# Attention of a two-layer trunk: the reciprocal sum moves from the exponentials to the matrix that they are transposed with

## The chip, the cores and the metric

The kernel runs on one core of a Trainium2 chip. The metric is the device time of one execution in microseconds, the lower the better. PE is the matrix engine (PEld its weight loads, which the profile shows on their own), DVE the vector engine, ACT the scalar engine, POOL the GpSimd engine, SP the engine that issues most DMAs. The matrix engine has two clock levels, 1.2 and 2.4 GHz; the granted clock is given as a share of the higher one.

## The reference, cut to what matters

A trunk of two layers over 256 latent and 256 context tokens of width 1024. Layer 0 mixes tokens by Fourier groups and a bidirectional state-space scan, layer 1 by attention; each is followed by a squared-ReLU MLP of width 4096. Only the attention of layer 1 is touched. It has 16 heads of 64: 8 window heads (4 query heads share one key head, a band mask, and a sink logit that takes part in the sum but has no value vector) and 8 neighbourhood heads (a bias per pair of positions). Every latent query sees the 256 latent and the 256 context keys:

```
s_loc  = where(valid, q k^T * scale, NEG_INF)      # or + bias
s_ctx  = q kc^T * scale
p      = softmax(concat([s_loc, s_ctx, s_sink], -1), -1)
o      = p_loc @ v + p_ctx @ vc
```

So a row of 512 exponentials is divided by its sum, and the result multiplies the values. All of it is in 32-bit floats.

## The kernel before

The kernel is written by hand, engine by engine. The function `script()` returns one list of steps. Every engine walks that same list and emits its own part of each step in that order, with semaphores between engines; nothing reorders instructions afterwards. For every result in PSUM (the eight banks that the matrix engine writes) a small table names the bank, what fills it and what frees it.

The attention is cut into 16 units, `ATTN`: a pair of heads (`par` 0 and 1) by one of two blocks of 128 queries. Index `i` below is the unit, 0 to 15; units 0 to 7 are window heads, 8 to 15 neighbourhood heads. The steps of a unit are:

- S (PE, L2383): scores of both heads, 128 queries by 512 keys, one PSUM bank each. Four banks are used in turn, two per unit.
- max (DVE, L1882 to L1893): adds mask or bias in PSUM, takes the row maximum, turns its sign.
- exp (ACT, L1393): reads the bank, writes `prob` (128 queries by 512 keys in SBUF, three units deep) as exp(s - max) and the row sum beside it.
- scale (DVE, L1902, L1905, L1909): adds the sink (window heads), takes the reciprocal, and multiplies `prob` of each head in place by it, one instruction of 128x512 per head, `prob_done` + 1 for each.
- PT (PE, L2392): for each head four transposes of 128x128, so that keys lie on partitions. `prob` is loaded as the weights, the identity matrix streams past. One bank per head (2 and 3).
- PT on ACT (L1404): copies both banks to `pT` in SBUF.
- O (PE, L2410): values times `pT`, four chunks of keys for each head, the two heads beside each other in the array.
- ohi, olo (ACT L1408, DVE L1914): every second unit, splits the output into a high and a low part for the output projection.

In the steady part one round of the script, for `j`, reads

```
for kind, i in (("S", j + 2), ("ohi", j - 2), ("max", j + 1), ("scale", j), ("olo", j - 2), ("exp", j + 1), ("PT", j), ("O", j - 1)):
```

so PE runs S of unit j+2, PT of unit j, O of unit j-1; DVE runs max of j+1, scale of j and, every second round, olo; ACT runs ohi, exp of j+1 and the copies of PT of j. The first units start beside the input projection of the layer, whose last products (L1936) end shortly before. When the attention ends, PE makes a row of gate values (L2222, step `grow`) and the output projection and the second MLP follow, in which nearly all products are of the three-fold form at L1936 and L1943.

Two other places use the matrix engine on plain 32-bit operands of the size that matters here. In layer 0, step `y` ends with three products whose moving operand is the identity, added into a bank (L2204), in each of 16 steps:

```
ins = mm(ps[:, b, P * i:P * i + P], ycomb[:, n % 2, P * i:P * i + P], ident, start=False, stop=True, skip_group_check=True)
```

and step `cb` makes four products of 128x128 by 128x128 in each of 4 steps (L2168), directly after the transposes of step `toks` (L2151, L2152; `nc.tensor.transpose`, as in PT).

Of the kernel before, what the change touches and what calls it, by code (L numbers as in the profile page):

```python
# [14 lines left out]
ALU = mybir.AluOpType  # L15
# [5 lines left out]
P = 128  # L21
# [3 lines left out]
T = SEQ + CTX  # L25
# [336 lines left out]
def trunk(nc, x, ctx, w_mod, vectors, w_ff1, w_ff2, w_in_even, w_dt, w_out_even, w_in_odd, rpb_na, w_out_odd,  # L362
# [171 lines left out]
    with ExitStack() as stack:  # L534
# [114 lines left out]
        bias = place("bias", [P, 2, 8, SEQ], offset=region + 16384)  # L649
        prob = place("prob", [P, 3, 2, T], offset=macc_at + 7680)  # L650
        pT = place("pT", [P, 2, 2, T], offset=vtok_end)
        assert vtok_end + 8 * 2 * T <= region + 16384
        fin = place("fin", [P, 2, D], offset=out_at)
        grow = place("grow", [P, D], offset=out_at + 2 * 4 * D)

# [10 lines left out]
        for name, w in (("cos", SEQ), ("sin", SEQ), ("perm", P), ("dup0", P), ("dup1", P), ("heads", P),  # L666
# [31 lines left out]
                 "wdthi_done wdtlo_done dtv_done dte_done dtln_done dt_done dtx_done uf_done vf_done pad_done acc_done "  # L698
                 "th_done xbc_done hs_done btok_done xdt_done xw_done ent_done seg_done g_done y_done zt_done gate_done gated "
                 "ysq_done mix_done mixhi_done hr_done hq_done hidhi_done hid_done qraw_done qn_done rope_done "  # L700
                 "vT_done vtok_done kd_done max_done exp_done rs_done prob_done pT_done pv_done ohi_done "
                 "tap_done xskip_done fin_done out_in vhi_done vsplit_done pair_used zr_done cvec_done crow_done ccol_done shift_done shh_done shl_done uo_done ahi_done").split()
        S = {n: sem(n) for n in names}
        (arow_done, rows_out, coef_half, grow_done, htok_done, unit_done, sines_done, hv_done, mfull_done, dtrow_done, acc_sq, tmp_sq, mu_used, row_done, mcol_done, modc_done, sil_done, hi_done, lo_done, c0_in, dft_in, xsq_done, xrms_done, xr_done, xn_done, xnt_done, xu_done, c1_in, vec_in, wdt_in, bias_in, dve_seq, act_seq,
# [2 lines left out]
         uf_done, vf_done, pad_done, acc_done, th_done, xbc_done, hs_done, btok_done, xdt_done, xw_done, ent_done, seg_done,  # L707
         g_done, y_done, zt_done, gate_done, gated, ysq_done, mix_done, mixhi_done, hr_done, hq_done, hidhi_done,
         hid_done, qraw_done, qn_done, rope_done, vT_done, vtok_done, kd_done, max_done,
         exp_done, rs_done, prob_done, pT_done, pv_done, ohi_done, tap_done, xskip_done, fin_done, out_in, vhi_done, vsplit_done, pair_used, zr_done, cvec_done, crow_done, ccol_done, shift_done, shh_done, shl_done, uo_done, ahi_done) = (S[n] for n in names)  # L710
        x_in = [sem(f"x_in{t}") for t in range(NCH)]

        def signalled(what):
# [698 lines left out]
        def _(dve):  # L1412
# [51 lines left out]
            for st in steps:  # L1464
# [371 lines left out]
                elif k == "hnorm":  # L1836
                    dve.wait_ge(hs_done, qk_n[st[1:]] + 1)
                    dve.wait_ge(qraw_done, qk_n[st[1:]] + 1)
                    x_ = ktile(*st[1:])
                    key = ("hstat",) + st[1:]  # L1840
                    r_, b = rms_of(key), jobs[key][0]
                    c_ = u32[:, 0, 0:odd_tokens[st[1:]]]
                    if qk_n[st[1:]]:
                        dve.wait_ge(qn_done, qk_n[st[1:]])
                    v.tensor_tensor(c_, r_, r_, ALU.mult).then_inc(signal(dve_seq), 1)
                    dve.wait_ge(*latest())
                    v.scalar_tensor_tensor(out=c_, in0=ps[:, b, 0:odd_tokens[st[1:]]], scalar=HD * EPS, in1=c_, op0=ALU.add, op1=ALU.mult).then_inc(signal(hv_done), 1)
                    v.scalar_tensor_tensor(out=x_, in0=x_, scalar=vt[:, 2, g_q[st[1]]:g_q[st[1]] + 1],
                                           in1=r_, op0=ALU.mult, op1=ALU.mult).then_inc(signal(dve_seq), 1)
                    dve.wait_ge(hv_done, qk_n[st[1:]] + 1)  # L1850
                    v.tensor_scalar(c_, c_, -0.5 / HD, 1.5, ALU.mult, ALU.add).then_inc(signal(dve_seq), 1)
                    dve.wait_ge(*latest())
                    v.tensor_tensor(x_, x_, c_, ALU.mult).then_inc(signal(qn_done), 1)
                elif k == "rot":
                    x_ = ktile(*st[1:])[:, 0:SEQ]
                    b = jobs[st][0]
                    dve.wait_ge(*filled(st))
                    dve.wait_ge(*latest())
                    v.tensor_tensor(rp[:, 0, :], x_, cuts["cos"], ALU.mult).then_inc(signal(dve_seq), 1)
                    v.tensor_tensor(rp[:, 1, :], ps[:, b, 0:SEQ], cuts["sin"], ALU.mult).then_inc(freeing(st), 1)  # L1860
                    dve.wait_ge(*latest())
                    v.tensor_tensor(x_, rp[:, 0, :], rp[:, 1, :], ALU.add).then_inc(signal(rope_done), 1)
                elif k == "dup":
                    b = jobs[st][0]
                    dve.wait_ge(*filled(st))
                    v.tensor_copy(kdup[:, st[1], :], ps[:, b, :]).then_inc(signal(kd_done), 1)
                elif k == "max":
                    i = st[1]
                    t, qt = ATTN[i]
                    b = jobs[st_S(i, 0)][0]  # L1870
                    for par in range(2):
                        dve.wait_ge(*filled(st_S(i, par)))
                    if t < 4:
                        o = P * (1 - qt)
                        cut_ = ps[:, b:b + 2, o:o + P]
                        add = cuts["win"][:, None, P * qt:P * qt + P].broadcast_to([P, 2, P])
                    else:
                        if t == 4:
                            dve.wait_ge(bias_in, 16 * 8)
                        cut_ = ps[:, b:b + 2, 0:SEQ]  # L1880
                        add = bias[:, qt, 2 * (t - 4):2 * (t - 4) + 2, :]
                    v.tensor_tensor(cut_, cut_, add, ALU.add).then_inc(signal(dve_seq), 1)  # L1882
                    dve.wait_ge(*latest())
                    v.tensor_reduce(sm[:, 3, i % 3, :], ps[:, b:b + 2, :], AX, ALU.max).then_inc(signal(dve_seq), 1)  # L1884
                    dve.wait_ge(*latest())
                    if t < 4:
                        sinks = bc[:, 120 + 2 * t:122 + 2 * t]
                        v.tensor_tensor(sm[:, 3, i % 3, :], sm[:, 3, i % 3, :], sinks, ALU.max).then_inc(signal(dve_seq), 1)
                        dve.wait_ge(*latest())
                        v.tensor_scalar(sm[:, 0, i % 3, :], sm[:, 3, i % 3, :], -1.0, None, ALU.mult).then_inc(signal(dve_seq), 1)  # L1890
                        v.tensor_tensor(sm[:, 4, i % 3, :], sinks, sm[:, 3, i % 3, :], ALU.subtract).then_inc(signal(max_done), 1)
                    else:
                        v.tensor_scalar(sm[:, 0, i % 3, :], sm[:, 3, i % 3, :], -1.0, None, ALU.mult).then_inc(signal(max_done), 1)  # L1893
                elif k == "scale":
                    i = st[1]
                    t, qt = ATTN[i]
                    row = lambda r: sm[:, r, i % 3, :]
                    for par in range(2):
                        dve.wait_ge(*exponential_done(i, par))
                    src = row(1)  # L1900
                    if t < 4:
                        v.tensor_tensor(row(5), row(1), row(2), ALU.add).then_inc(signal(dve_seq), 1)  # L1902
                        dve.wait_ge(*latest())
                        src = row(5)
                    v.reciprocal(row(4), src).then_inc(signal(rs_done), 1)  # L1905
                    dve.wait_ge(*latest())
                    for par in range(2):
                        pr = prob[:, i % 3, par, :]
                        v.tensor_scalar(pr, pr, sm[:, 4, i % 3, par:par + 1], None, ALU.mult).then_inc(signal(prob_done), 1)  # L1909
                elif k == "olo":  # L1910
                    t = st[1]
                    dve.wait_ge(ohi_done, t + 1)
                    b, _ = jobs[("Opair", t)]
                    v.tensor_tensor(a_lo[:, t, 0:SEQ], ps[:, b, 0:SEQ], a_hi[:, t, 0:SEQ].bitcast(F32), ALU.subtract).then_inc(signal(split_done), 1)  # L1914
                elif k == "out":
                    dve.wait_ge(grow_done, 2)
                    dve.wait_ge(htok_done, 4)
                    for q in range(4):
                        t, c_ = q // 2, 512 * (q % 2)
                        dve.wait_ge(*filled(("acc", q)))  # L1920
                        v.tensor_tensor(nt[:, q % 2, :], ps[:, B_TOK[q], :], grow[:, c_:c_ + 512], ALU.mult).then_inc(signal(dve_seq), 1)
                        dve.wait_ge(*latest())
                        v.tensor_tensor(fin[:, t, c_:c_ + 512], nt[:, q % 2, :], fin[:, t, c_:c_ + 512], ALU.add).then_inc(signal(fin_done), 1)
# [3 lines left out]
        def _(pe):  # L1927
# [42 lines left out]
            for st in steps:  # L1970
# [413 lines left out]
                elif k == "PT":  # L2384
                    i = st[1]
                    for par in range(2):
                        pe.wait_ge(prob_done, 2 * i + par + 1)
                        b = jobs[st + (par,)][0]
                        if free_before[st + (par,)]:
                            pe.wait_ge(*emptied(st + (par,)))  # L2390
                        for kk in range(NCH):
                            ins = nc.tensor.transpose(ps[:, b, P * kk:P * kk + P], prob[:, i % 3, par, P * kk:P * kk + P], ident)  # L2392
                        ins.then_inc(filling(st + (par,)), 1)
                elif k == "O":
                    i = st[1]
# [89 lines left out]
```

## Time and profile before

| | us |
|---|---|
| median of 3 runs | 1194.53 |
| lowest, highest | 1194.1, 1195.05 |
| the profiled execution, its own time | 1193.66 |
| its span, first to last instruction | 1191.9 |

Of the span PE is busy 1159.9 us (97%), its weight loads 930.6 (78%), DVE 840.6 (71%), ACT 616.9 (52%), POOL 84.4 (7%). Matmuls are pipelined: a row of the trace gives the time from a matmul's start to its modelled end, which overlaps the next one, so the distance between starts says more than the duration. Times inside the span are microseconds from its start. In a timeline, neighbouring instructions of one kind are merged into a row: start, length, engine, line, operands, how many (x), and in brackets the idle time of the engine before it with what ended it.

### The profile page before, as it was taken

What the parts mean: (1) busy time and instruction counts of PE and PEld (TensorE: products, weight loads), DVE (VectorE), ACT (ScalarE), POOL (GpSimd) and SP (SyncE); (2) the same over time, 40 slices, a digit from 0 to 9 for tenths busy, and PEclk for the clock granted to TensorE, in tenths of its full rate; (3) what the DMA queues carried; (4) which work ended last, traced back from release to release, by engine and by line L of the source; (5) the groups of instructions that cost most, each with busy time, mean ns of one, the idle gap of its engine ahead of it and who ended that gap; (6) DMA issues with size and microseconds to landing.
All of it is one profiled execution on the core that took longest, in us unless ns stands there. A gap on an engine that the chain in (4) does not pass through costs nothing.

```text
span 1191.9 us, 17207 instructions
## 1 busy us (share of the span) xinstructions
PE 1159.9 (97%) x6430; PEld 930.6 (78%) x6430; DVE 840.6 (71%) x1208; ACT 616.9 (52%) x1074; POOL 84.4 (7%) x73
## 2 busy tenths in 40 slices
PE   5999999999999999999999999999999999999998
PEld 3677677787867787887887887887887579998997
DVE  4563687988978666893882882897777977654655
ACT  5541485949584547622422422446855777654552
POOL 0000101010100042000000000043000004000000
PEclk9999999999999999999999999999999999999999
DMA  9855543342422233644634634631343005555554
GB/s 362 345 182 216 191 143 100 106 125 80 124 80 82 90 125 117 219 146 142 232 123 142 229 119 144 229 122 66 126 136 128 2 4 175 162 192 177 194 182 154
DMA packets 49893, 179.13 MB, mean 150 GB/s; under 512 B 5216, under 2 KB 7584, under 8 KB 47776
## 3 DMA queue, kind: packets, MB, share of 16 engines
q1 hardware_dynamic: 49536, 177.66, 43.5%
q8 instruction: 43, 0.70, 0.2%
q10 hardware_dynamic: 288, 0.56, 0.1%
q14 instruction: 26, 0.21, 0.1%
HBM read 177.05 MB, written 1.15 MB: 150 GB/s over the span
## 4 chain that ended last, share of the span: by engine, by line
PE 84%; DVE 8%; DMA 3%; ACT 3%; issue 2%; SPq 0%; DVEq 0%; ACTq 0%
PE ps L1936 54%; PE ps L1943 9%; PE ps L2230 7%; PE ps L2028 2%; PE ps L2200 2%; DVE sm L1884 2%; DMA mhalf<-in_w_mod 1%; PE ps L1959 1%; PE ps L2187 1%; PE ps L2204 1%; PE ps L2141 1%; DVE ps L1882 1%; DVE prob L1909 1%; DMA xload<-in_ctx 1%; ACT w_hi L1049 1%
## 5 line engine op out<-in xcount | busy, mean ns | idle before, releaser
L1419 DVE TENSOR_TENSOR w_lo<-raw,w_hi 128x1024 fp32r<-128x1024 f32 x206 | 262.6, 1275 | 91.2 <-ACT w_hi L1049 91.2
L1049 ACT ACTIVATE w_hi<-raw 128x1024 fp32r<-128x1024 f32 x206 | 216.8, 1053 | 192.2 <-DMA raw<-in_w_ff 155.6
L1936 PE MATMUL ps<-a_hi,w_hi 128*128 128x512 f32 (+1 forms) x820 | 299.1, 365 | 0.0
L1936 PE MATMUL ps<-a_hi,w_lo 128*128 128x512 f32 (+1 forms) x820 | 288.9, 352 | 0.0
L1936 PE MATMUL ps<-a_lo,w_hi 128*128 128x512 f32 (+1 forms) x820 | 288.7, 352 | 0.0
L1936 PEld LDWEIGHTS ps<-a_hi,w_hi 128*128 128x128 f32 x820 | 155.1, 189 | 26.0 <-issue 2.7
L1936 PEld LDWEIGHTS ps<-a_lo,w_hi 128*128 128x128 f32 x820 | 155.2, 189 | 23.1 <-issue 1.0
L1936 PEld LDWEIGHTS ps<-a_hi,w_lo 128*128 128x128 f32 x820 | 155.0, 189 | 21.3
L1936 PE MATMUL ps<-b_hi,w_hi 128*128 128x512 f32 x304 | 119.2, 392 | 0.0
L1936 PE MATMUL ps<-b_lo,w_hi 128*128 128x512 f32 x304 | 118.5, 390 | 0.0
L1936 PE MATMUL ps<-b_hi,w_lo 128*128 128x512 f32 x304 | 118.3, 389 | 0.0
L1797 DVE SCALAR_TENSOR_TENSOR macc<-mring,silc,macc 128x1536 f32<-128x1536 f32 x56 | 103.5, 1889 | 0.0
L1369 ACT ACTIVATE hr<-ps 128x512 f32<-128x512 f32 x30 | 17.9, 596 | 98.4 <-PE ps L1936 65.7
L1943 PE MATMUL ps<-a_hi,w_hi 128*128 128x512 f32 (+1 forms) x188 | 67.0, 356 | 1.5 <-DVE a_lo L1758 0.4
L1936 PEld LDWEIGHTS ps<-b_hi,w_hi 128*128 128x128 f32 x304 | 57.1, 188 | 14.4 <-DVE hT L1823 1.9
L1936 PEld LDWEIGHTS ps<-b_hi,w_lo 128*128 128x128 f32 x304 | 57.1, 188 | 11.9
L1936 PEld LDWEIGHTS ps<-b_lo,w_hi 128*128 128x128 f32 x304 | 57.1, 188 | 11.6
L1943 PE MATMUL ps<-a_lo,w_hi 128*128 128x512 f32 (+1 forms) x188 | 64.9, 345 | 0.0
L1943 PE MATMUL ps<-a_hi,w_lo 128*128 128x512 f32 (+1 forms) x188 | 64.9, 345 | 0.0
L1629 DVE SCALAR_TENSOR_TENSOR cacc<-cpad,vec,cacc 128x512 f32<-128x512 f32 x80 | 60.1, 752 | 5.9 <-ACT cacc L1223 0.7
L1275 ACT ACTIVATE ey<-ey,acum 128x128 f32<-128x128 f32 x192 | 59.3, 389 | 0.0
L1823 DVE SCALAR_TENSOR_TENSOR hT<-ps,mod,hT 128x256 f32<-128x256 f32 x64 | 27.9, 477 | 43.0 <-PE ps L1936 43.0
(289 smaller groups left out, 1762.3 us busy)
## 6 DMA issues: line engine op xcount, KB each, us to landing
raw<-in_w_ff SPq DMA_DIRECT2D x128, 512.0 KB, 3.5
mring<-in_w_mod SPq DMA_DIRECT2D x32, 768.0 KB, 5.3
raw<-in_w_in_even SPq DMA_DIRECT2D x36, 512.0 KB, 5.8
mring<-in_w_mod SPq DMA_DIRECT2D x16, 1024.0 KB, 5.1
ey<-acum_rows SPq DMA_DIRECT2D x32, 384.0 KB, 5.0
raw<-in_w_in_odd SPq DMA_DIRECT2D x18, 512.0 KB, 3.5
mhalf<-in_w_mod SPq DMA_DIRECT2D x16, 512.0 KB, 9.6
raw<-in_w_out_even SPq DMA_DIRECT2D x16, 512.0 KB, 3.5
```

Source lines behind the costliest of these rows:

```text
L1049: nc.scalar.activation(w_hi[:, u % RING, :, :], raw[:, u % RING, :, :], ACT.Copy).then_inc(hi_done, 1)
L1275: nc.scalar.activation(ey[:, di, r, :], ey[:, di, r, :], ACT.Relu, scale=-1.0, bias=acum[:, st[3], head_col(st) + r:head_col(st) + r + 1]) ...
L1419: v.tensor_tensor(w_lo[:, u % RING, :, :], raw[:, u % RING, :, :], w_hi[:, u % RING, :, :].bitcast(F32), ALU.subtract).then_inc(lo_done, 1)
L1629: v.scalar_tensor_tensor(out=acc, in0=cpad[:, n % 2, :, w:w + SEQ], scalar=convwT[:, w, t:t + 1], in1=acc, op0=ALU.mult, op1=ALU.add).then ...
L1797: ins = v.scalar_tensor_tensor(out=macc[i][:, :], in0=row, scalar=weight, in1=macc[i][:, :], op0=ALU.mult, op1=ALU.add)
L1823: ins = v.scalar_tensor_tensor(out=hs, in0=ps[:, b, SEQ * i:SEQ * i + SEQ], scalar=mod[:, L, 5 * KT + m, i:i + 1], in1=hs, op0=ALU.mult, o ...
L1884: v.tensor_reduce(sm[:, 3, i % 3, :], ps[:, b:b + 2, :], AX, ALU.max).then_inc(signal(dve_seq), 1)
L1936: ins = mm(out_ap, w_[:, n % RING, k, :], (x_[k][:, 0:ntok] if type(x_) is list else x_[:, k, 0:ntok]), start=(k == 0 and j == 0), stop=(k ...
L1943: ins = mm(outs[i], w_[:, tiles_[i] % RING, k, :], (x_[k][:, 0:ntok] if type(x_) is list else x_[:, k, 0:ntok]), start=(k == 0 and j == 0) ...
L2028: ins = mm(ps[:, LEAD_BANKS[i], 0:ntok], w_[:, slot + i, kk, :], x_[:, kk, c_:c_ + ntok], start=(kk == 0 and q == 0), stop=(kk == KT - 1 a ...
L2200: mm(ps[HD * par:HD * par + HD, b, P * i:P * i + P], xdt[:, di, ch, HD * r:HD * r + HD], ey[:, di, r, :], start=(i == 0 and di == 0), stop ...
L2230: ins = mm(ps[:, B_TOK[q], :], x_[:, m, P * t:P * t + P], moving_rows(w_, u, half), start=(begin and j == 0), stop=(end and j == 2))
```

## The change

The exponentials stay unscaled. Instead of multiplying `prob` by the reciprocal sum, DVE multiplies the identity by it, which gives a diagonal matrix `wdiag` for each head (128x128, three units deep), and PE multiplies `prob` by that diagonal with an ordinary matmul where it transposed with the identity. Column q of the result is the row q of `prob` times its reciprocal, the same numbers as before. DVE waits, from unit 3 on, until PT of three units earlier is done before it overwrites a diagonal. The semaphore `prob_done` is renamed `diag_done`; steps, banks and the order of instructions on every engine stay as they are. `mm` is `nc.tensor.matmul`.

```
-        assert vtok_end + 8 * 2 * T <= region + 16384
+        assert vtok_end + 8 * 2 * T + 4 * 3 * 2 * P <= region + 16384
+        wdiag = place("wdiag", [P, 3, 2, P], offset=vtok_end + 8 * 2 * T)
...
                     v.reciprocal(row(4), src).then_inc(signal(rs_done), 1)
                     dve.wait_ge(*latest())
+                    if i >= 3:
+                        dve.wait_ge(*filled(("PT", i - 3, 1)))
                     for par in range(2):
-                        pr = prob[:, i % 3, par, :]
-                        v.tensor_scalar(pr, pr, sm[:, 4, i % 3, par:par + 1], None, ALU.mult).then_inc(signal(prob_done), 1)
+                        v.tensor_scalar(wdiag[:, i % 3, par, :], ident, sm[:, 4, i % 3, par:par + 1], None, ALU.mult).then_inc(signal(diag_done), 1)
...
                     for par in range(2):
-                        pe.wait_ge(prob_done, 2 * i + par + 1)
+                        pe.wait_ge(diag_done, 2 * i + par + 1)
                         b = jobs[st + (par,)][0]
                         if free_before[st + (par,)]:
                             pe.wait_ge(*emptied(st + (par,)))
                         for kk in range(NCH):
-                            ins = nc.tensor.transpose(ps[:, b, P * kk:P * kk + P], prob[:, i % 3, par, P * kk:P * kk + P], ident)
+                            ins = mm(ps[:, b, P * kk:P * kk + P], prob[:, i % 3, par, P * kk:P * kk + P], wdiag[:, i % 3, par, :], start=True, stop=True)
                         ins.then_inc(filling(st + (par,)), 1)
```

## Rows read from the trace of the kernel before

**Rows 1.** Busy time by stretch: PE, PEld, DVE, ACT, POOL, granted clock, DMA share, GB/s.
```profile
927.00:976.00 49.00, 45.48 (x428) 30.41 (x427) 43.65 (x108) 38.46 (x100) 0.00 (x0) 1.00 0.01 2
```
**Rows 2.** Waits from 927.1 to 975.8: who for whom, total us, times, longest.
```profile
PEld ps L2392 <- DVE prob L1909: 13.2, 14, 1.5
...
PE ps L2392 <- DVE prob L1909: 2.9, 7, 1.2
```
**Rows 3.** Timeline of PE over the attention.
```profile
923.89 0.63 PE L2392 MATMUL ps<-c,prob 128*128 128x128 f32 x4 [0.45 <-DVE u L1847]
924.45 1.13 PE L2383 MATMUL ps<-kdup,qT 64*128 64x512 f32 x4
...
927.16 1.09 PE L2392 MATMUL ps<-c,prob 128*128 128x128 f32 x8
...
953.46 1.13 PE L2383 MATMUL ps<-kT,qT 64*128 64x512 f32 x4
954.52 1.09 PE L2392 MATMUL ps<-c,prob 128*128 128x128 f32 x8
955.54 1.09 PE L2410 MATMUL ps<-pT,vtok 128*64 128x128 f32 x16
956.56 1.13 PE L2383 MATMUL ps<-kT,qT 64*128 64x512 f32 x4
...
970.78 1.09 PE L2392 MATMUL ps<-c,prob 128*128 128x128 f32 x8 [1.23 <-DVE prob L1909]
...
973.85 1.97 PE L2410 MATMUL ps<-pT,vtok 128*64 128x128 f32 x32
975.75 1.09 PE L2222 MATMUL ps<-c,mod 128*128 128x128 f32 x8
```
**Rows 4.** Timeline of DVE over two rounds.
```profile
955.78 1.22 DVE L1884 TENSOR_REDUCE sm<-ps 128x2 f32<-128x1024 f32 x1
...
957.32 0.88 DVE L1909 TENSOR_SCALAR prob<-prob,sm 128x512 f32<-128x512 f32 x2
958.12 0.69 DVE L1882 TENSOR_TENSOR ps<-ps,bias 128x512 f32<-128x512 f32 x1
...
960.38 0.88 DVE L1909 TENSOR_SCALAR prob<-prob,sm 128x512 f32<-128x512 f32 x2
961.18 0.42 DVE L1914 TENSOR_TENSOR a_lo<-ps,a_hi 128x256 fp32r<-128x256 f32 x1
...
962.24 1.23 DVE L1884 TENSOR_REDUCE sm<-ps 128x2 f32<-128x1024 f32 x1
```
**Rows 5.** Groups by form, whole span: busy us, mean ns, idle before.
```profile
L2204 PE MATMUL ps<-c,ycomb 128*128 128x128 f32 x96 | 15.0, 292 | 1.7 <-DVEq L1723 1.7
L2392 PE MATMUL ps<-c,prob 128*128 128x128 f32 x128 | 17.7, 280 | 6.0 <-DVE prob L1909 2.9 <-ACT vtok L1267 2.4 <-DVE u L1847 0.4
```
**Rows 6.** Timeline of PE in layer 0, products with the identity.
```profile
306.22 0.94 PE L2204 MATMUL ps<-c,ycomb 128*128 128x128 f32 x6
306.99 0.81 PE L2187 MATMUL ps<-hent,xbc 128*128 128x384 f32 x2
```
**Rows 7.** Timeline of PE in layer 0, transposes and then ordinary products.
```profile
322.01 0.49 PE L2151 MATMUL ps<-c,xbc 128*128 128x128 f32 x3
322.34 0.27 PE L2152 MATMUL ps<-c,xbc 128*128 128x128 f32 x1
322.45 1.06 PE L2168 MATMUL ps<-xbc 128*128 128x128 f32 x8
```
**Rows 8.** Groups of DVE by form, whole span.
```profile
L1909 DVE TENSOR_SCALAR prob<-prob,sm 128x512 f32<-128x512 f32 x32 | 14.1, 483 | 0.6
L1851 DVE TENSOR_SCALAR u<-u 128x256 f32<-128x256 f32 x8 | 2.3, 285 | 0.0
L1468 DVE TENSOR_SCALAR vec<-vec 128x120 f32<-128x120 f32 x1 | 0.2, 223 | 4.0 <-DMA vec<-in_vectors 4.0
```

## What the change will do to the time

> **What bounds the kernel now.** I read the page first: PE is busy 97% of the span, so outside the attention the time is set by products that this change does not touch. Then busy time by stretch: in the 49 us from 927 to 976, which hold the units 1 to 15 of the attention, PE is busy 45.48 us and DVE 43.65 us, ACT 38.46 us, DMA moves nearly nothing, and PE's clock is granted in full (1.00, the 2.4 GHz level) [rows 1]. So two engines are nearly full there, and which of them sets the pace is for the waits and the timelines to say. The longest wait of the stretch is PE's for L1909, DVE's multiplication of `prob`: 13.2 us in 14 waits on the side of the weight loads, of which 2.9 us leave the matmuls idle [rows 2]. The reader is to see that it is DVE that is late, but by little.
>
> How little is worked out from PE's own timeline [rows 3]. Where nothing is waited for, PT takes 1.02 us from its start to that of O (954.52 to 955.54), O takes 1.02 (955.54 to 956.56), and S takes 1.06 (953.46 to 954.52): 3.10 us per unit. On DVE the row maximum starts at 955.78 and, two rounds later, at 962.24 [rows 4]: 3.23 us per round. From the start of PT of unit 1 (927.16) to the `grow` step (975.75) are 48.59 us. PE's work in it without a wait is 15 PT of 1.02 (15.3), O of units 0 to 13 (14 x 1.02 = 14.3), O of the last two together (973.85 to 975.75, 1.9) and S of units 4 to 15 (12 x 1.06 = 12.7), in sum 44.2 us. So all waits of PE in the attention are worth 4.4 us, the largest of them 1.23 us at the end (unit 14). That is all that a faster DVE can give.
>
> **What it takes from DVE.** Removed are 32 multiplications of 128x512 of 483 ns; put in their place are 32 of 128x128. The trace has the same operation at 128x120 (223 ns) and at 128x256 (285 ns) [rows 8]; I take 0.22 us, on the side of the nearest size. Two neighbours overlap: the pair now holds DVE from 957.32 to 958.12, 0.80 us [rows 4]. With 0.17 to 0.22 us for each of the small ones the pair is 0.35 to 0.45 us, a gain of some 0.4 us per round, 3.23 to about 2.8 us. It is a real saving, and it goes to an engine that then is not the bound.
>
> **What it adds to PE.** PT of a unit is eight calls before and eight after, but the calls are of another kind. The 128 calls of PT (16 units x 8) left 128 records [rows 5]: a transpose is one pass. Step `y` makes three calls of `mm` with the identity as the moving operand in each of 16 steps, 48 calls, and left 96 records: an ordinary 32-bit product is two passes, whatever stands in the moving operand. It is the same form that PT gets, 128x128 weights and 128 moving columns. The distance of passes: four transposes take 0.44 us from 322.01 to 322.45, 0.11 each; the eight passes of the four calls behind them last 1.06 us of which the last one's own length is some 0.28, so (1.06 - 0.28) / 7 = 0.112 each [rows 7]. A pass costs the same, and there are twice as many.
>
> So the passes of PT go from 8 x 0.11 = 0.88 to 16 x 0.112 = 1.79 us. The group has edges besides, from the wait before and the hand-over behind: now 1.02 - 0.88 = 0.14 us. For an ordinary product the edge can be larger: the six passes at L2204, which also stand behind a wait, take 0.77 us from start to the next group's start (306.22 to 306.99), 0.10 more than 6 x 0.112 [rows 6]. Lowest is 1.79 (no edge), then 1.93 (edge as now), 2.03 (both edges); highest is 16 passes at the mean of L2204, 0.128 each, plus 0.14: 2.19. I take 1.98, in the middle of those two with an edge. PT costs 0.96 us more per unit, and a unit's work on PE is 1.98 + 1.02 + 1.06 = 4.06 us.
>
> **Who waits then.** DVE with 2.8 us and ACT (38.46 us over 15 rounds, 2.6 us each) both have over a microsecond to spare in a round of 4.06, so the 4.4 us of waits should go. The tightest place is the diagonal of unit j. Its DVE chain begins when S of unit j+1 has ended: from the addition of the bias (958.12) to the start of the scaling (960.38) 2.26 us, then 0.4 for the diagonals [rows 4], so 2.7 us; PE meanwhile does PT of unit j-1, O of j-2 and S of j+2, 4.06 us. There is 1.3 us of slack, a third of a microsecond less where olo comes first. At the end, where unit 14 now waits 1.23 us because no S follows any more, PE has PT and O to do, 3.0 us against 2.7: nearly or just covered. The exponentials of unit j+2 stand behind ACT's copies of unit j, which now end 1 us later, but their diagonal is wanted two rounds on. The new wait on DVE is for PT three units back, which was issued before everything that DVE waits for in that round; behind it are the two diagonals and the next max, and I cost it at nothing. If the cover were gone, its price would be that of the rival below that keeps the waits.
>
> **Sum.** After: 15 x 1.98 = 29.7, and O and S as before, 14.3 + 1.9 + 12.7 = 28.9, so 58.6 us against 48.59: +10.0 us. Unit 0 stands before this stretch: its first half runs inside an idle time of PE, its second half (923.89 to 924.45, 0.56 us, four calls) is followed by S, a last transposition of values, S and PT with no wait [rows 3], so its 0.5 us more pass through. Together +10.5 us. Behind the attention PE goes on without a break into `grow` and the output projection, whose first weights are already split; nothing there gives time back. The profiled execution has its own time of 1193.66 us, 1.8 above its span, and lies 0.9 under the median; 1193.66 + 10.5 = 1204.2 for a profiled execution, and 1205.0 for the median.
>
> On transposes, the Trainium skill's page "TensorE: Matmul & The Clock Gate" (section "Terms") says that the transpose mode is four times faster for 32-bit data. This trace shows a ratio of two (16 passes of 0.112 against 8 of 0.11). By the page the passes of PT would be 3.5 us long and the median about 1231 us; where page and rows differ I go by the rows, and leave the page's case as one of the rivals.
>
> **Rivals.**
> 1. The waits stay. If PE's waits in the attention come not from DVE's load but from a chain that runs through PE itself (PT, ACT's copy, ACT's exp, DVE's diagonal), they move along with the longer PT: 15 x 0.96 + 0.5 = +14.9 us, 1209.4. For it: ACT's queue does put exp behind the copies. Against it: that chain spans two rounds, and in the trace PE waits for L1909 alone. 12%.
> 2. The other side: PT stays as long as it is. If an ordinary product with such a diagonal were one pass, the saving of DVE would decide: DVE's 2.8 us fall under PE's 3.10, the 4.4 us of waits go, and the time is 1190.1. The point from which it decides: PT under 1.02 + 4.4/15 = 1.31 us; above that the kernel gets slower. For it: the operand is diagonal and the call count is the same. Against it: L2204 has the identity itself there, and leaves two records for each call. 5%, of which 1% for a result within the measurement.
> 3. An ordinary product costs four transposes, not two. Then PT is 8 x 4 x 0.11 + 0.14 = 3.66 us, 15 x 2.64 - 4.4 + 1.3 = +36.5 us, 1231. Against it are the 96 records and their distance. 3%.
>
> **How the numbers follow.** My forecast has 80%. Its own range: PT from 1.79 to 2.19 us gives 15 x 0.77 - 4.4 + 0.4 = +7.6 to 15 x 1.17 - 4.4 + 0.6 = +13.8, so 1202.1 to 1208.3. The range that I give reaches a little to either side, down to 1201.8 and up to rival 1, 1209.5. A change of 0.2% (2.4 us) is about what a measurement of this kernel can tell from none; all cases but rival 2 lie far above it. Slower 95%, same 1%, faster 4%.
>
> **What would show it.** Twice as many records of PT at L2394 of the changed kernel, 256 for 128, a hair over 0.11 us apart, and PT to O close to 1.98 us; a round of 4.06 us on PE; the wait for the diagonals gone or nearly so; DVE's new instructions near 0.22 us, and DVE idle for over a microsecond in each round; the stretch from PT of unit 1 to `grow` 58.6 us long, and everything before and behind it as it was. I am wrong if the records of PT stay 128, if PE still waits for DVE by more than a microsecond or two in sum, or if the part behind the attention changes its length.

## The result, and the profile after

The changed kernel takes 1205.47 us (median of 4 runs, 1203.91 to 1206.5) against 1194.79 for the kernel before (4 runs, one more than in the table ahead of the prediction, 1194.1 to 1195.87): 0.88% slower, ratio 1.0088 with a 95% interval of 1.0076 to 1.0101. The prediction was 1205.0. The profiled execution has 1203.91 us and a span of 1202.1, 10.25 and 10.2 us more than before; it is the shortest of the four, the others have 1205.22 to 1206.5.

First the busy time by stretch, after the change (columns as in [rows 1]); the stretch is eleven microseconds longer than that of before because the attention is:

```profile
927.00:987.00 60.00, 60.00 (x554) 45.84 (x551) 40.27 (x109) 40.47 (x101) 0.00 (x0) 1.00 0.01 1
```

PE is busy all of the 60 us, DVE 40.27 of them; before it was 45.48 and 43.65 of 49 [rows 1]. Two nearly full engines have become one full engine. The waits of the same stretch (who for whom, us in total, times, longest), whole lines from the list:

```profile
ACT pT L1405 <- PE ps L2394: 13.7, 28, 1.3
PEld ps L2394 <- issue: 8.5, 12, 0.8
DVE ps L1883 <- PE ps L2385: 8.3, 12, 1.3
...
PEld ps L2394 <- DVE wdiag L1911: 1.7, 3, 0.8
```

The direction is turned round: where PE waited for DVE [rows 2], DVE now waits for PE's scores, up to 1.3 us at a time, and ACT for PE's PT. What is left of PE's wait for the diagonals, 1.7 us, is on the weight loads alone, and no row of PE's matmuls carries an idle time for it. PE's timeline (start, length) of PT of unit 1, two rounds of the steady part, and the end, beside [rows 3]:

```profile
927.70 2.05 PE L2394 MATMUL ps<-wdiag,prob 128*128 128x128 f32 x16
...
956.15 2.05 PE L2394 MATMUL ps<-wdiag,prob 128*128 128x128 f32 x16
958.14 1.09 PE L2412 MATMUL ps<-pT,vtok 128*64 128x128 f32 x16
959.16 1.13 PE L2385 MATMUL ps<-kT,qT 64*128 64x512 f32 x4
960.22 2.05 PE L2394 MATMUL ps<-wdiag,prob 128*128 128x128 f32 x16
...
986.37 1.09 PE L2224 MATMUL ps<-c,mod 128*128 128x128 f32 x8
```

PT has 16 records a unit instead of 8, takes 1.98 to 1.99 us to the start of O (1.02 before), O and S take 1.02 and 1.06 as before, and the round is 4.07 us. No row carries an idle time. From PT of unit 1 to `grow` are 58.67 us (48.59 before). DVE over one round, beside [rows 4]:

```profile
956.37 0.70 DVE L1883 TENSOR_TENSOR ps<-ps,bias 128x512 f32<-128x512 f32 x1 [1.32 <-PE ps L2385]
...
958.64 0.48 DVE L1911 TENSOR_SCALAR wdiag<-c,sm 128x128 f32<-128x128 f32 x2
959.72 0.42 DVE L1916 TENSOR_TENSOR a_lo<-ps,a_hi 128x256 fp32r<-128x256 f32 x1 [0.59 <-ACT a_hi L1409]
960.43 0.70 DVE L1883 TENSOR_TENSOR ps<-ps,bias 128x512 f32<-128x512 f32 x1 [0.29 <-PE ps L2385]
```

The pair of DVE instructions has gone from 0.88 to 0.48 us from first start to last end, and what DVE gained went into idle time. The groups by form, beside [rows 5] and [rows 8]:

```profile
L2394 PE MATMUL ps<-wdiag,prob 128*128 128x128 f32 x256 | 33.0, 282 | 2.4 <-ACT vtok L1268 2.4
...
L1911 DVE TENSOR_SCALAR wdiag<-c,sm 128x128 f32<-128x128 f32 x32 | 7.7, 284 | 0.6
```

Outside the attention little moved: PT of unit 1 starts 0.54 us later (927.70 for 927.16), and from `grow` to the end of the span are 215.7 us, 216.2 before. So 0.54 + 10.08 - 0.42 = 10.2 us, the whole difference.

### The profile page after: what moved, and what is told of

Read it like the earlier page. It is cut to its first block, busy times and chain, and to the rows that moved or that the text cites. A ratio compares the mean times of both kernels' runs of the same rounds, so it can differ in the third digit from the quotient of the medians.

```text
span 1202.1 us, 17476 instructions
## 1 busy us (share of the span) xinstructions
PE 1174.2 (98%) x6558; PEld 947.2 (79%) x6558; DVE 835.8 (70%) x1208; ACT 617.3 (51%) x1074; POOL 84.4 (7%) x73
## 4 chain that ended last, share of the span: by engine, by line
PE 88%; DVE 4%; ACT 3%; DMA 3%; issue 2%; SPq 0%; DVEq 0%; ACTq 0%
PE ps L1938 54%; PE ps L1945 9%; PE ps L2232 7%; PE ps L2394 3%; PE ps L2030 2%; PE ps L2202 2%; PE ps L1961 1%; DMA mhalf<-in_w_mod 1%; PE ps L2412 1%; PE ps L2385 1%; PE ps L2189 1%; PE ps L2206 1%; PE ps L2143 1%; DMA xload<-in_ctx 1%; PE ps L2133 1%
```

## The experiments

The theory: in the attention the longer of PE's work and DVE's work sets the round, and the change lengthens PE's by doubling the passes of PT. Its rivals were waits that run through a chain and do not melt away (rival 1 of the prediction), a part of the cost on DVE's side (diagonals or their new wait), and an edge that comes with the form and not the pass count. Medians, with the kernel before measured beside each (e1, e3 and e5 leave out all or part of the division by the sums):

| run | what it does | median us | before | ratio, 95% |
|---|---|---|---|---|
| e1_diag_transpose | DVE's part alone | 1191.58 | 1194.49 | 0.9962 to 0.9985 |
| e2_scale_matmul | PE's part alone | 1205.18 | 1194.49 | 1.0074 to 1.0102 |
| e5_one_of_four | 10 passes | 1195.96 | 1195.11 | 0.9996 to 1.0014 |
| e3_two_of_four | 12 passes | 1198.46 | 1194.49 | 1.0018 to 1.0038 |
| e6_one_diagonal | wait on the unit before | 1205.15 | 1195.11 | 1.0070 to 1.0101 |
| e8_load2 | 0.92 us more on DVE | 1206.09 | 1195.11 | 1.0078 to 1.0109 |
| e8_load4 | 1.85 us more on DVE | 1215.92 | 1195.11 | 1.0160 to 1.0191 |
| e4_fp32r | one pass, less precise | 1192.68 | 1194.49 | 0.9974 to 0.9992 |
| g1_repeat | e1 once more | 1191.80, one run | 1194.37 | |
| g2_constant | constant for the sums | 1206.67, one run | 1194.37 | |
| j4_fp32r_filled | e4, idle time filled | 1191.85 | 1194.54 | 0.9965 to 0.9984 |
| k3_filled | e1, idle time filled | 1190.52, one run | 1194.60 | |

### The two halves of the change apart

DVE's part alone, as a difference to the changed kernel:

```
-  ins = mm(ps[...], prob[...], wdiag[:, i % 3, par, :], start=True, stop=True)
+  ins = nc.tensor.transpose(ps[...], prob[...], ident)
```

> DVE's part of the change alone: DVE makes the diagonals as in the changed kernel, PE transposes the unscaled exponentials with the identity as in the kernel before (the division by the sums is left out). Theory (the time in the attention is the larger of PE's work and DVE's): 128 records of PT, PT to O 1.02 us, PE's round 3.10 us against 2.9 on DVE, the waits of 4.4 us shrink to some 0.8 (unit 14 only), median 1191.2. Rival 1 (PE's waits come from a chain through ACT's copies and exponentials): waits as before less 0.3 us a chain, 1194 to 1195. Rival 3 (the diagonals or their wait cost PE something by themselves): slower than the kernel before.

PE's part alone, as a difference to the kernel before (DVE scales `prob` in place):

```
-  ins = nc.tensor.transpose(ps[...], prob[...], ident)
+  ins = mm(ps[...], prob[...], ident, start=True, stop=True)
```

> PE's part alone: DVE scales prob in place as before (0.80 us a pair instead of 0.48), PE uses an ordinary matmul with the identity. Theory: 256 records, PT to O 1.98 us whatever the moving operand holds, DVE's round of 3.23 us hidden under PE's 4.06, at most 0.2 us more at unit 14: 1205.5 to 1205.8. Rival (DVE's shorter work is part of the changed kernel's time): 0.32 us a round more, 1210.

The halves have opposite signs. PE's alone is the whole slowdown, 1205.18 against 1205.47 of both, with the plain identity as the moving operand. So it is the kind of instruction, not what the diagonal holds, and DVE's longer scaling costs nothing under PE's 4.06 us. DVE's alone is 2.9 us faster, 0.4 us less than expected; its timeline of PE at the end of the attention:

```profile
955.25 1.09 PE L2394 MATMUL ps<-c,prob 128*128 128x128 f32 x8
...
958.35 1.09 PE L2394 MATMUL ps<-c,prob 128*128 128x128 f32 x8
...
970.50 1.09 PE L2394 MATMUL ps<-c,prob 128*128 128x128 f32 x8 [0.71 <-DVE wdiag L1911]
...
975.47 1.09 PE L2224 MATMUL ps<-c,mod 128*128 128x128 f32 x8
```

A round is 3.10 us, PE's bare work. The waits of the matmuls left in the stretch are unit 14's 0.71 us and one of 0.21 at 939.71. From PT of unit 1 (930.08) to `grow` are 45.4 us, 3.2 less than before. So nearly all of PE's waits were DVE's load and melted; rival 1, which expected 1194 to 1195, falls. In this profile PT of unit 1 also starts 2.9 us late, for which see the last section.

### The dose on PE

One or two of the four calls of each head as ordinary matmuls, the others as transposes:

```
   for kk in range(NCH):
-      ins = mm(ps[...], prob[...], wdiag[:, i % 3, par, :], start=True, stop=True)
+      if kk < 2:      # or 1
+          ins = mm(ps[...], prob[...], wdiag[:, i % 3, par, :], start=True, stop=True)
+      else:
+          ins = nc.tensor.transpose(ps[...], prob[...], ident)
```

> As the changed kernel, but only two of the four calls of PT per head are ordinary matmuls with the diagonal, the other two transpose with the identity (their part of the division is left out). Theory: 12 passes, PT to O 1.50 us, so 15.5 x 0.48 = 7.4 us above the run with transposes alone, less half a microsecond of wait at unit 14: 1198.2. Rival (changing between the two kinds of product within a group costs an edge of 0.05 to 0.1 us each time): PT 1.6 to 1.7 us, 1200 to 1201.5.

> As the changed kernel with one of the four calls of PT per head an ordinary matmul with the diagonal, three transposes with the identity (their division left out): 10 passes. Theory: PT to O 1.29 us (1.02 and 1.53 were measured with 8 and 12 passes), PE's round 3.37 us, work of PE 15 x 1.29 + 28.9 = 48.3 against the 48.6 that the stretch lasts in the kernel before: the break-even point, 1194.5, within 1 us. Rival 1 (part of the waits stays): 1196 to 1198.

With two of four, PE's timeline of one PT:

```profile
953.45 0.71 PE L2395 MATMUL ps<-wdiag,prob 128*128 128x128 f32 x4
954.00 0.38 PE L2397 MATMUL ps<-c,prob 128*128 128x128 f32 x2
954.22 0.61 PE L2395 MATMUL ps<-wdiag,prob 128*128 128x128 f32 x4
954.66 0.38 PE L2397 MATMUL ps<-c,prob 128*128 128x128 f32 x2
954.98 1.09 PE L2415 MATMUL ps<-pT,vtok 128*64 128x128 f32 x16
```

Two calls give four records. PT is 1.53 us; with one of four it is 1.29. Two, four and eight of the eight calls of a unit exchanged lengthen PT from 1.02 to 1.29, 1.53 and 1.98 us, and the stretch from PT of unit 1 to `grow` from 45.4 to 48.9, 52.1 and 58.7 us. All three fit, to 0.01 us, 0.115 us for each call (two passes of 0.112 for one of 0.109) and 0.05 us once, at the front of the group. The rows show where these edges lie. The first four passes, behind S, take 0.55 us to the next row and the four in the middle 0.44, so an ordinary product has 0.11 us at the front; the last two transposes take 0.32 against 0.22, so the hand-over to O costs 0.10. Changing forms inside a group costs nothing.

The medians follow less evenly: 1191.6, 1196.0, 1198.5 and 1205.5 us, steps of 4.4, 2.5 and 7.0, 13.9 in all. By the lengths of PT in 15.5 units (unit 0 counts half), less the waits that go, the steps would be 3.7, 3.5 and 6.8. The run with 10 passes is the one out of line. It is at the break-even that the prediction had put at 1.31 us of PT and cannot be told from the kernel before (0.9996 to 1.0014). It is 1.5 us over the expected 1194.5, outside the margin of 1 us that I had given it and at the lower end of what rival 1 would give, 1196 to 1198. Its trace speaks against rival 1: between PT of unit 1 (928.65) and `grow` (977.55) the only row of PE with an idle time has 0.44 us. What its profile lost lies before: PT of unit 1 starts 1.5 us later than in the kernel before, most of it in a stretch of low clock (last section), and the kernel before was itself 0.6 us higher beside this run.

### DVE's slack and the new wait

One pair of diagonals instead of three (and the index 0 wherever `wdiag` had `i % 3`):

```
-  wdiag = place("wdiag", [P, 3, 2, P], ...)
+  wdiag = place("wdiag", [P, 1, 2, P], ...)
-  if i >= 3:
-      dve.wait_ge(*filled(("PT", i - 3, 1)))
+  if i >= 1:
+      dve.wait_ge(*filled(("PT", i - 1, 1)))
```

> As the changed kernel with one pair of diagonals instead of three: DVE waits in each unit for PT of the unit just before. Theory (the wait has cover even then): PT of unit j-1 ends 1.98 us after S of unit j+1, DVE reaches the diagonal of j 2.2 us after it, so nothing changes, 1205.0 to 1205.8. Rival (the wait on DVE is part of what the change costs): one to two us more per round, 1220 and above.

Added load on DVE, 2 or 4 instructions that nobody reads, before each pair of diagonals:

```
+  for q in range(2):      # or 4
+      v.tensor_scalar(rp[...], c1[:, 0:T], 1.0, None, ALU.mult).then_inc(signal(dve_seq), 1)
+      dve.wait_ge(*latest())
```

> As the changed kernel with two idle-running DVE instructions of 128x512 before each pair of diagonals, each waited for (some 0.47 us each, 0.95 us per unit). Theory (PE's 4.06 us a round is the bound, DVE has over a microsecond to spare): DVE 3.9 us a round stays under it, 1205.5 to 1206.5, the most of it at unit 14. Rival (DVE still counts in the round): 14 us more, 1219.

> The same with four such instructions, 1.9 us per unit. Theory: DVE's 2.9 + 1.9 = 4.8 us a round pass PE's 4.06 and set the pace: 0.7 to 0.8 us a round, 1214 to 1218, and PE waits for the diagonals again.

Even the strictest form of the new wait costs nothing, 1205.15. Two added instructions lengthen DVE's work by 0.92 us in each unit (their start to that of the diagonals, in the trace) and the kernel stays at 1206.1. PE's matmuls wait in two places only: 0.42 us at unit 2 (932.06) and 0.67 at unit 14, where no S covers the chain:

```profile
978.76 1.09 PE L2415 MATMUL ps<-pT,vtok 128*64 128x128 f32 x16
980.53 2.05 PE L2397 MATMUL ps<-wdiag,prob 128*128 128x128 f32 x16 [0.67 <-DVE wdiag L1914]
```

With four, 1.85 us more, the cover is gone, the kernel is at 1215.9, and PE's matmuls wait for the diagonals again:

```profile
PEld ps L2397 <- DVE wdiag L1914: 19.9, 13, 2.0
PE ps L2397 <- DVE wdiag L1914: 9.8, 13, 1.8
```

DVE sets the pace there: in the steady part two rounds take 9.35 us by PE's PT (963.68 to 973.03), 4.68 each, so 1.85 us more on DVE lengthened a round of 4.06 by 0.6. DVE therefore has some 1.2 us to spare in a round of the changed kernel, whose time its work does not set.

### One pass in another type, and the DVE instruction by itself

```
-  prob = place("prob", [P, 3, 2, T], offset=macc_at + 7680)
+  prob = place("prob", [P, 3, 2, T], F32R, offset=macc_at + 7680)
-  wdiag = place("wdiag", [P, 3, 2, P], offset=vtok_end + 8 * 2 * T)
+  wdiag = place("wdiag", [P, 3, 2, P], F32R, offset=vtok_end + 8 * 2 * T)
```

> As the changed kernel, with prob and the diagonals stored in the fp32r type that the kernel's large products use, which is less precise: one pass for each product. Theory: 128 records of PT; the rate of the kernel's other fp32r products (some 0.12 us apart with 256 columns) gives 0.06 us a pass if columns set it and up to 0.11 if the weight loads do, PT 0.7 to 1.1 us; then DVE's 2.9 us or PE's 2.8 to 3.1 set the round: 1190 to 1191.5. Rival (an ordinary product needs two passes also in this type): 1205.5. Rival 3 (waits stay): 1194.

```profile
L2394 PE MATMUL ps<-wdiag,prob 128*128 128x128 f32 x128 | 18.6, 288 | 3.5 <-ACT vtok L1268 2.4 <-DVE wdiag L1911 0.9 <-DVE u L1848 0.2
```

128 records again, PT 1.04 us, and the time is under that of the kernel before, by 0.17% (interval 0.08 to 0.26%). This is the idea of the change in a form that pays, at the price of storing the exponentials and the diagonals less precisely. It is 1.2 us above the upper end of what I expected. The single pass is no shorter than a 32-bit transpose (1.04 us for PT against 1.02), near the upper end of the 0.7 to 1.1 us that I had allowed. Its records are 0.11 us apart with 128 columns, and the kernel's fp32r products with 256 columns are 0.12 apart: here the columns alone do not set the rate. What does was not tested.

```
-  v.tensor_scalar(wdiag[...], ident, sm[:, 4, i % 3, par:par + 1], None, ALU.mult)
+  v.tensor_scalar(wdiag[...], ident, 0.01, None, ALU.mult)
```

> The changed kernel with the constant 0.01 in place of the column of reciprocal sums as factor of the diagonals (the division is left out). I had put the new DVE instruction at 0.22 us and it took 0.284. Theory: an operand that is read for each partition costs about 0.06 us over a constant, so here 0.22 us for 128x128; rival: a 128x128 instruction simply takes 0.28. The time stays near 1205 either way.

```profile
L1911 DVE TENSOR_SCALAR wdiag<-c 128x128 f32<-128x128 f32 x32 | 5.8, 224 | 0.5
```

224 ns with a constant, 284 with the per-partition operand (one profile of 32 instructions; this kernel leaves the division out). The instructions with 512 columns that were added above also have a constant and take 427 ns, where L1909 took 483. The two rows from which I had taken the 0.22 us [rows 8, the second and third] both have constants; L1909, the instruction that was removed, had such an operand.

## Why the prediction was right

- An ordinary product in PT is two passes a call: shown. 256 records, and PE's half alone has the whole slowdown.
- PT to O 1.98 us, 0.96 more: 1.98 to 1.99 in the changed kernel. That the middle of 1.93 and 2.03 was hit to a hundredth is partly luck. The value with both edges counted the front of the group twice: the 0.10 us that L2204 shows stand in place of the 0.05 at the front of a transpose group and do not come on top of them. With the 0.11 at the front and the 0.10 at the hand-over that the dose run shows, 16 x 0.112 becomes 2.0, the measured time within the rounding.
- O and S as before, round of 4.06: shown (4.07).
- All 4.4 us of PE's waits go: shown in the changed kernel, where PE has no idle row from PT of unit 1 to `grow`. They come back when DVE is loaded by 1.85 us more. With transposes kept (e1) 3.2 of the 4.4 went.
- DVE idle for over a microsecond in each round: on average. Of 40.66 us in ten rounds (939.89 to 980.55) DVE is busy 29.04, so 1.16 are idle; the waits are 1.3 us in one round and 0.9 in the next, where olo falls.
- The stretch 58.6 us: 58.67. Unit 0, 0.5 us: 0.54. Nothing given back behind: the tail is 0.4 us shorter, which no step of the prediction has and no run explains; the other profiles of unfilled kernels have tails of 215.6 to 216.9.
- DVE's new instruction 0.22 us: wrong, 0.284, because the rows that I took had a constant as factor. The pair is 0.48 us instead of 0.35 to 0.45. It cost nothing, since DVE is not the bound.
- The median: 1205.0 against 1205.47. The rise was put at 10.5 us and is 10.25 by the profiled executions and 10.68 by the medians. The runs of the changed kernel scatter by 2.6 us, so the closeness of this figure proves less than the terms above do.
- The new wait at nothing: shown, even at its strictest.

The other side (rival 2: one pass, 1190.1) failed at its condition. Its sum would have been 1.5 us too low: DVE's half with transposes gives 1191.6, since 0.9 us of waits stay, unit 14's above all, and low clock takes a part (last section). The cost of four transposes in rival 3 is refuted by the records. On the Trainium skill's rules: "TensorE: Matmul & The Clock Gate" (section "Terms") has the transpose four times faster for 32-bit data; here an ordinary product takes twice a transpose (1.79 us of passes against 0.88), so the measurement decides against the figure. The Trainium skill's page "Perfetto Trace Analysis" (section "Transposes") asks that logical transposes be made as transposes and not as ordinary matmuls; the runs agree: the 128 calls made as ordinary matmuls with the identity cost 10.7 us (1205.18 against 1194.49).

## What to carry to other kernels

Folding a scale into a transposition turns the transpose into an ordinary product. With plain 32-bit operands that was two passes for one here; in fp32r it was one, and PT as long as before. Before an operation is moved from one engine to another, sum up both engines' work per round without their waits. Here 3.10 us on PE stood against 3.23 on DVE, and PE's waits were 4.4 us in all, so relief of DVE could bring 4.4 us at most, and any load on PE over 0.3 us a unit had to lose. Count the records of a form that already runs in the kernel against its calls in the source: that gave the doubling, and with the two sums the sign.

## What was not expected of the hardware

PE's granted clock falls for some microseconds early in the attention in some executions, from 1.00 (2.4 GHz) to 0.50 (1.2 GHz). Run e1 (stretch, then the columns as in [rows 1]; the clock is the third number from the right):

```profile
920.00:923.00 3.00, 0.58 (x6) 0.38 (x5) 1.24 (x3) 2.77 (x8) 0.00 (x0) 1.00 0.54 171
923.00:926.00 3.00, 2.59 (x10) 1.53 (x12) 2.56 (x10) 1.19 (x2) 0.00 (x0) 0.56 0.01 4
926.00:930.00 4.00, 4.00 (x12) 1.22 (x8) 2.04 (x5) 1.18 (x2) 0.00 (x0) 0.50 0.00 0
930.00:935.00 5.00, 5.00 (x52) 3.66 (x52) 4.29 (x11) 4.46 (x14) 0.00 (x0) 0.98 0.02 5
```

Before it falls PE has waited 2.4 us for ACT (until 922.92); then it runs at the 1.2 GHz level until about 930, and PT of unit 1 starts at 930.08 instead of 927.16. The kernels before and after have the same 2.4 us of idle time and show 1.00 there in their profiles, so I asked whether it belongs to the kernel.

> The kernel of run e1_diag_transpose once more, unchanged, for a second profile. In e1's profile PE's granted clock stood at 0.5 from about 924 to 930 us, after 2.4 us in which PE waited for ACT; in the profiles of the kernels before and after it stayed at 1.00. If that belongs to the kernel, it is there again and PT of unit 1 starts near 930; if it comes and goes between executions, this profile may show it at 1.00 and PT of unit 1 near 927.

The clock fell again, but for a shorter time (0.57, then 0.89 from 926 to 930). In all, 7 of the 12 profiles of kernels with that idle time show a fall (e1, e4, e5, e6, e8_load4, g1, g2), 5 do not (before, after, e2, e3, e8_load2), and there is no part of the change that goes with it. Two kernels put two idle-running matmuls there (their results are read by nobody):

```
+  if i == 0:
+      ...      # a wait until the bank is free
+      for q in range(2):
+          mm(ps[:, B_Y, :], ident, c0[:, 0:4 * P], start=True, stop=True)
```

> e1_diag_transpose with two idle-running 32-bit matmuls of 512 columns (about 1.7 us) on PE in its 2.4 us of idle time before PT of unit 0. If the idle time is what the clock falls after, the granted clock stays at 1.00 from 923 to 930 in this profile; if not, it falls as in e1.

> e4_fp32r (the whole computation, prob and diagonals in fp32r) with two idle-running 32-bit matmuls of 512 columns (about 1.7 us) on PE in its 2.4 us of idle time before PT of unit 0. PT 1.04 us, PE's round 3.12, DVE's 2.9. If the idle time is what the clock falls after, it stays at 1.00 from 923 to 930 and the median is 1190 to 1191.5 against 1192.7 for e4; without effect of the filling: 1192.7. Either way under the kernel before.

```profile
920.00:923.00 3.00, 2.29 (x10) 1.02 (x9) 1.28 (x2) 2.66 (x6) 0.00 (x0) 1.00 0.54 175
923.00:926.00 3.00, 2.55 (x16) 1.33 (x14) 2.73 (x10) 1.19 (x2) 0.00 (x0) 1.00 0.03 5
```

Both kept 1.00 there (the rows are of k3_filled). k3_filled is at 1190.5 in one run; j4_fp32r_filled at 1191.85, whose interval against the kernel before (0.9965 to 0.9984) overlaps that of e4 (0.9974 to 0.9992). It has the lowest median of the kernels that leave nothing out.

That the filling keeps the clock up is not shown. Near the start of the kernel, while PE waits for weights (1.9 us until 25.8 and 0.7 until 27.1 in the kernel before), there is a second place where the clock can fall. The same stretch in the kernel before and in e1:

```profile
27.00:33.00 6.00, 5.86 (x40) 2.80 (x43) 4.19 (x7) 1.94 (x4) 0.00 (x0) 0.72 1.05 387
27.00:33.00 6.00, 5.07 (x48) 2.32 (x49) 4.47 (x8) 2.21 (x5) 0.00 (x0) 1.00 1.05 388
```

Of the 12 profiles without filling, the six that keep 1.00 there all fall in the attention, and of the six that fall there (the five without a fall in the attention, and g2) one falls in the attention as well. Both filled profiles fall there, so by the count of the others they may well have kept the clock in the attention without any filling. What links the two places no run shows. The early fall does not delay the attention: PT of unit 0 starts at 922.7 to 923.6 us in the profiles with it and at 922.6 to 923.2 in those without. Nor does filling one gap protect the rest: in the profile of j4_fp32r_filled PE waits 1.8 us for DVE at 1141.5, the clock is at 0.55 from 1144.6 to 1148.4, and this execution takes 1195.7 us, the longest of its ten.

The fall in the attention is worth 1.2 to 2.9 us by the start of PT of unit 1. Three profiled executions of e1's kernel, one of them filled, order themselves by it: PT of unit 1 at 927.14, 928.72 and 930.08 (k3, g1, e1), and the times are 1190.52, 1191.80 and 1193.18. How often timed executions lose this stays open. It is a possible reason why e1, e4 and e5 came out 0.4, 1.2 and 1.5 us over their expectations, and why the runs of one kernel mostly scatter by two microseconds and more; differences of a microsecond between medians should be read with that in mind.
